# A decode-and-prefill layer on one core: the sample's sequences spread over the prompt's attention at every tenth half block in place of every eighth

## The chip, the cores and the metric

The kernel runs on one NeuronCore of a Trainium2 chip. The metric is the device time of one execution in microseconds (us). TensorE, VectorE, ScalarE and GpSimd have a queue each and work it off in program order; SyncE issues most of the transfers. They are tied to each other by semaphores only.

## The reference, cut to what matters

One layer of a hybrid decoder is applied to a prompt (1 sequence of 2048 tokens) and to a sample (8 sequences of 4 new tokens, each with a cache of keys and values). Only the attention is touched by the change. For the prompt:

```
for window, dilation in ((128, 1), (512, 4), (2048, 16)):
    # queries of one residue class, 128 at a time, against the 128 keys before and their own 128
    sc = einsum(q_block, k_window) * dh ** -0.5, masked to the band
    m = max(sc); p = exp(sc - m); l = sum(p); o = (p / l) @ v_window
outs of the three configurations merged by softmax of their log-sums
```

For each of the 8 sample sequences, the 4 new queries of 8 heads see, in the same three configurations, 129 strided keys each:

```
kg, vg = k_all[:, idx], v_all[:, idx]
sc = einsum('bthd,btjhd->bthj', q, kg) * dh ** -0.5
lse = logsumexp(sc); p = exp(sc - lse)
outs.append(einsum('bthj,btjhd->bthd', p, vg))
```

Around it stand the input projection and the RWKV-7 mixing (before), and the output projection, the mixture of experts and the final norm (behind).

## The kernel before, in words

The stages run one behind another. `attention` (L1266) is the third. Its prompt part has 48 blocks of 128 queries: 16 of dilation 1, 16 of dilation 4 (four residue classes of four), 16 of dilation 16 (sixteen classes of one). A block is done in two halves of four heads each, so there are 96 half blocks, u = 0 to 95. The first block of a class has no keys before it, and its halves use 128 keys in place of 256; from u = 64 on all are such small ones.

In a step u TensorE does: the scores of half block u+2 (`score`, L1474), the turning of the exponentials of u (`turn_p`, L1494), the weighting of u-1 by the values (`weigh`, L1508 and L1509), up to u = 26 in even steps a turning of the prompt's keys (`turn_x`, L1456), and in odd steps what there is of the sample (`sample`). VectorE does: mask and extremum of u+2 (`mask_min`, L1667), half of the copy of u's turned exponentials (`p_copy`, L1675), the sample's part. ScalarE does: exponentials of u+1 (L1576), the other half of the copy (L1583), the copy of the output of u-1 (L1590), the sample's exponentials and the issue of most of its transfers (`sample_loads`, L1602). In odd steps TensorE waits in `sample(u)` for both copies of u.

A sequence b of the sample is tied to the half block `at(b) = first_at + period * b`, with `first_at` 13:

- GpSimd multiplies keys and queries in three products (L1425, tiles `att_s_prd` and `ahead_feat` in turn: two buffers). Product i waits until the head sum i-2 has read its buffer.
- VectorE's head sums (L1698) stand at u = at(b)-6, -5 and -3, scale and mask (L1702) at -1.
- TensorE turns the scores at at(b) (L1518), VectorE takes the maxima, ScalarE the exponentials.
- TensorE turns the exponentials back at at(b)+4 (L1522, L1523), VectorE copies them (L1722, L1723), GpSimd spreads them over the nine key tiles (`by_tile`, L1433, tile `att_s_lm`).
- TensorE weighs the values at at(b)+6 (`weigh_sample`): 18 passes of L1529, 128 rows by 512 columns, and 2 of L1530 with 4 rows. VectorE keeps each head's own columns (L1727, L1729).
- The values of b are loaded by ScalarE's queue at at(b+1)-9, -8 and -7, the keys of b+1 at at(b)-6, -4 and -2, its queries at at(b)-5.

GpSimd's queue is written in this order:

```
for b in range(B):
    for j in range(3):
        product(b, j)
    if b >= 1:
        by_tile(b - 1)
by_tile(B - 1)
```

and TensorE's weighing waits for the values and for `by_tile`:

```
pe.wait_ge(sv_ld, 64 * b + 64)
pe.wait_ge(s_lm, b + 1)
```

The first turning of half block u behind a sample's step (`turn_p`) waits until VectorE has read the shared PSUM bank `t_ps[1]`. SyncE stores the sample's results at block (at(b) + 11) // 2.

Of the kernel before, what the change touches and what calls it, by code (L numbers as in the profile page):

```python
# [1265 lines left out]
def attention(nc, X, QT, ident, mask, spare, x_ld, q_ld, c_in, k_in, v_in, qkv_s, cache_k, cache_v, masks_s, o_out, m_out, os_out, ms_out):  # L1266
# [6 lines left out]
    NU = 2 * NBK  # L1273
    NV, NX, NO, NSC = 5, len(X), 3, 3
    B, N = cache_k.shape[0], cache_k.shape[1]
    at_new, first_at, period = 7, 13, 8
    at = lambda b: first_at + period * b
    with ExitStack() as ctx:
        sb = lambda n, s: ctx.enter_context(nc.sbuf_tensor(f"att_{n}", s, F32))
# [1476 lines left out]
def hybrid_layer(nc, a, consts, outs):  # L2756
# [34 lines left out]
                att_X, att_QT[:], att_ident[:], att_mask[:], kc_p, qt_p, ident, consts["band"], att_x_ld, att_q_ld, att_c_in)  # L2791
    clear_semaphores(nc)
    attention(nc, att_X, att_QT, att_ident, att_mask, rwkv_F[0], att_x_ld, att_q_ld, att_c_in, kc_p, vc_p, qkv_s, a["cache_att_k"], a["cache_att_v"], consts["sample"], o_p, m_p, o_s, m_s)
    early.close()
    clear_semaphores(nc)
# [50 lines left out]
```

## Time and profile before

| | |
|---|---|
| median of 3 runs | 3448.79 us (3446.48 to 3475.65) |
| the profiled execution | 3453.1 us, span of its instructions 3451.3 us |
| TensorE busy (matmul) | 3146.2 us, 91% |
| VectorE, ScalarE, GpSimd busy | 1318.3, 1013.0, 338.4 us |
| mean granted clock of TensorE | 0.951 |
| attention stage | about 1579 to 2036 us |

Times below are counted from the span's start. The durations and waits come from the one profiled execution, so they are set against its 3453.1 us. A granted clock of 1.00 is 2.4 GHz, 0.50 is 1.2 GHz. TensorE's matmuls overlap a little in the records, so the start of the next group is the safer end of a group. Every fp32 matmul is recorded as two passes, a turning (transpose) as one.

### The profile page before, as it was taken

Reading aid. Unit: us, or ns where it says so; the run is one execution under the profiler, and the core shown is the slowest. Engines: PE = TensorE matmul, PEld = TensorE weight load, DVE = VectorE, ACT = ScalarE, POOL = GpSimd, SP = SyncE. Lnnn points to the kernel's source line nnn. Section 1 sums busy time; section 2 is a strip of 40 time slices with the busy share of each in tenths; the row PEclk is TensorE's granted clock in tenths of the full one; section 3 lists DMA queues with packets and bytes.
Section 4 is the critical chain, followed back from the end, with each engine's and each line's share of the span. In section 5 each row is a group of like instructions: output and inputs, shape, how many; then the busy total and the mean of one; then the engine's idle time right before and its main releaser. Section 6 shows DMA issues by size and latency. Waiting matters only on the chain. (4 is left out here: it accounts for less than half of the span.)

```text
span 3451.3 us, 74888 instructions
## 1 busy us (share of the span) xinstructions
PE 3146.2 (91%) x30921; PEld 2149.7 (62%) x30922; DVE 1318.3 (38%) x3229; ACT 1013.0 (29%) x2151; POOL 338.4 (10%) x351
## 2 busy tenths in 40 slices
PE   6999999999859988988999979996999999999990
PEld 4667666676458888877767765554555555555550
DVE  3455344553224443435655436664111111111117
ACT  3334433344122222225544433331111111111112
POOL 0000000000110000003333000001101001010104
PEclk9999999999979999999999859997999999999995
DMA  6111111111273333326666446423768786677658
GB/s 209 63 71 65 51 46 63 70 55 45 72 180 113 120 137 120 119 98 204 183 182 179 125 162 193 154 80 123 278 242 284 239 283 223 227 277 245 233 193 306
DMA packets 299029, 544.42 MB, mean 158 GB/s; under 512 B 98146, under 2 KB 122466, under 8 KB 292116
## 3 DMA queue, kind: packets, MB, share of 16 engines
q1 hardware_dynamic: 252860, 401.29, 34.6%
q10 hardware_dynamic: 25128, 66.26, 6.1%
q0 software_dynamic: 20784, 73.15, 5.8%
q8 instruction: 197, 3.23, 0.4%
q14 instruction: 60, 0.49, 0.0%
HBM read 400.66 MB, written 139.98 MB: 157 GB/s over the span
## 5 line engine op out<-in xcount | busy, mean ns | idle before, releaser
L307 PE MATMUL proj_main_ps<-proj_xt,proj_w 128*128 128x257 f32 x1536 | 351.1, 381 | 0.0
L307 PEld LDWEIGHTS proj_main_ps<-proj_xt,proj_w 128*128 128x128 f32 x1536 | 290.2, 191 | 41.1
L2544 PE MATMUL moe_y_ps<-moe_w,moe_ht 128*64 128x512 f32 x1312 | 301.2, 601 | 3.1 <-ACT moe_ht L2583 3.1
L2292 PE MATMUL out_proj_ps<-out_w,out_ct 128*128 128x512 f32 x544 | 241.6, 598 | 6.1 <-DMA out_w<-in_w_out_dram 6.1
L337 PE MATMUL proj_main_ps<-proj_w,proj_xt 128*128 128x512 f32 x512 | 225.3, 593 | 0.0
L2594 ACT ACTIVATE moe_sg<-moe_gate 128x256 f32<-128x256 f32 x82 | 31.4, 383 | 535.7 <-PE moe_gate L2528 535.7
L2544 PEld LDWEIGHTS moe_y_ps<-moe_w,moe_ht 128*64 128x64 f32 x1312 | 87.3, 137 | 158.6 <-issue 155.3
L2292 PEld LDWEIGHTS out_proj_ps<-out_w,out_ct 128*128 128x128 f32 x544 | 101.7, 192 | 121.8 <-issue 120.5
L2630 DVE COPY moe_y<-moe_y_ps 128x512 f32<-128x512 f32 x82 | 56.7, 691 | 313.8 <-PE moe_y_ps L2544 313.8
L1190 DVE COPY_PREDICATED rwkv_t<-ahead_rwkv_cons,rwkv_level_ps 128x512 f32<-128x512 uint32 (+1 forms) x168 | 109.1, 660 | 175.7 <-PE rwkv_level_ps L908 175.4
L337 PEld LDWEIGHTS proj_main_ps<-proj_w,proj_xt 128*128 128x128 f32 x512 | 97.2, 190 | 108.4 <-issue 107.0
L1667 DVE CUSTOM_DVE_ANT_0 att_sc<-att_s_ps,ahead_mask 128x256 f32<-128x256 f32 (+1 forms) x384 | 117.2, 361 | 118.4 <-PE att_s_ps L1474 118.4
L908 PE MATMUL rwkv_level_ps<-rwkv_t,rwkv_w 64*64 64x64 f32 x2688 | 153.2, 221 | 2.7 <-issue 2.7
L2528 PE MATMUL moe_up<-moe_w,moe_xt 128*64 128x256 f32 x1344 | 154.3, 382 | 0.0
L2528 PE MATMUL moe_gate<-moe_w,moe_xt 128*64 128x256 f32 x1344 | 152.2, 379 | 0.0
L2579 ACT COPY moe_xt<-moe_xt_ps 128x512 f32<-128x512 f32 x83 | 48.6, 585 | 343.4 <-PE moe_xt_ps L2521 343.4
L2528 PE MATMUL moe_gate<-kept_first_gate,moe_xt 128*64 128x256 f32 x1280 | 147.5, 384 | 1.4 <-ACT moe_xt L2579 1.4
L2528 PE MATMUL moe_up<-kept_first_up,moe_xt 128*64 128x256 f32 x1280 | 146.9, 382 | 0.0
L1576 ACT ACTIVATE att_sc<-att_sc,att_nm 128x256 f32<-128x256 f32 (+1 forms) x384 | 145.6, 451 | 3.9 <-issue 3.1
L1509 PE MATMUL att_o_ps<-att_v,att_pt 128*128 128x65 f32 x768 | 142.0, 301 | 0.0
L2636 DVE TENSOR_TENSOR moe_hd<-moe_sg,moe_gate 128x256 f32<-128x256 f32 x82 | 34.6, 421 | 280.0 <-ACT moe_sg L2594 280.0
L1474 PE MATMUL att_s_ps<-att_kt,ahead_qt 64*128 64x256 f32 (+1 forms) x768 | 139.8, 493 | 0.9 <-DVE att_pt L1675 0.5
(362 smaller groups left out, 5535.3 us busy)
## 6 DMA issues: line engine op xcount, KB each, us to landing
moe_w<-in_expert_w_dram SPq DMA_DIRECT2D x64, 2048.0 KB, 9.6
y_rows<-rwkv_zero POOLq DMA_DIRECT2D x65, 512.0 KB, 4.8
kept_first_gate<-in_expert_w_dram SPq DMA_DIRECT2D x16, 2048.0 KB, 9.6
kept_first_up<-in_expert_w_dram SPq DMA_DIRECT2D x16, 2048.0 KB, 14.9
y_rows<-moe_y ACTq DMA_DIRECT2D x164, 128.0 KB, 6.0
ft_p<-proj_uf SPq DMA_DIRECT2D x32, 642.0 KB, 3.2
rwkv_feat<-ft_p SPq DMA_DIRECT2D x12, 1284.0 KB, 6.9
att_s_k<-in_cache_att_k_dram ACTq DMA_DIRECT2D x14, 1024.0 KB, 6.8
```

The lines of the kernel that those rows point to most:

```text
L307: last = mm(out[:, 0:w + 1], W[:, k, kind * C + m * P:kind * C + (m + 1) * P], XT[n % 2][:, k, 0:w + 1], start=(k == 0), stop=(k == KT - 1))
L337: last = mm(out[:], XT[n % 2][:, k, 1 + i // 2 * P:1 + (i // 2 + 1) * P], W[:, k, j * C:(j + 1) * C], start=(k == 0), stop=(k == KT - 1))
L908: last = mm(level_ps[g][part(c), hh * P + DH:(hh + 1) * P], W[g][part(c), hh, :], T[i % 3][part(c), h, DH:P], start=True, stop=True, skip_ ...
L1190: v.copy_predicated(T[i % 3][:, 4 * g:4 * g + 4, k0:P], wide(level(l)[:, k0:P], 4).bitcast(U32), four(level_ps[g][:])[:, :, k0:P]).then_in ...
L1474: last = mm(s_ps[u % 2][e][:, pl * 2 * P + k_from(u):(pl + 1) * 2 * P], QT[rows, q, q_at:q_at + d * (P - 1) + 1:d], KT[rows, q, k_at:k_at ...
L1509: last = mm(out, PT[u % 2][:, hl, 1, :], V[n % NV][:, h, :], start=first(u), stop=True, skip_group_check=True)
L1576: nc.scalar.activation(SC[u % NSC][:, hl, k0:], SC[u % NSC][:, hl, k0:], ACT.Exp, bias=NM[:, n, 4 * half + hl:4 * half + hl + 1], scale=-1 ...
L1667: v.tensor_tensor_reduce(SC[u % NSC][:, hl, k0:], s_ps[u % 2][e][:, pl * 2 * P + k0:(pl + 1) * 2 * P], mask[:, k0:], 1.0, 3e38, ALU.add, A ...
L2292: last = mm(proj_ps[j][:], CT[t % 2][:, k, :], W[:, k, 512 * j:512 * (j + 1)], start=(k == 0), stop=(k == KT - 1))
L2528: last = mm(bank[j * HB:(j + 1) * HB, 0:HF], XT[:, q, r * HB:(r + 1) * HB], W[:, k, j * HF:(j + 1) * HF], start=(k == 0), stop=(k == KT - ...
L2544: last = mm(py[j * HB:(j + 1) * HB, :], HT[:, c, r * HB:(r + 1) * HB], W2[s][:, k, j * 512:(j + 1) * 512], start=(k == 0), stop=(k == FE / ...
L2630: v.tensor_copy(Y[:], py[:]).then_inc(y_ev, 1)
```

## The change

One number in `attention`: the sequences are tied to half blocks 13, 23, ..., 83 in place of 13, 21, ..., 69. Everything that is placed by `at(b)` on the four engines and in the transfer queues moves with it; the last weighing goes from half block 75 to 89, and the last store of the sample's results from block 40 to block 47, the last one.

```
@@ -1273,7 +1273,7 @@
     NU = 2 * NBK
     NV, NX, NO, NSC = 5, len(X), 3, 3
     B, N = cache_k.shape[0], cache_k.shape[1]
-    at_new, first_at, period = 7, 13, 8
+    at_new, first_at, period = 7, 13, 10
     at = lambda b: first_at + period * b
```

## Rows read from the trace of the kernel before

**Rows 1.** Windows: us; busy PE, PEld, DVE, ACT, POOL; granted clock; DMA share; GB/s.

```profile
1598.90:1963.80 364.90, 361.33 (x2334) 269.00 (x2334) 217.46 (x753) 185.70 (x467) 122.88 (x32) 1.00 0.62 183
1964.00:2066.20 102.20, 78.53 (x389) 69.61 (x389) 41.01 (x201) 42.30 (x122) 0.95 (x1) 0.50 0.42 136
1938.98:1946.76 7.78, 7.78 (x62) 6.95 (x62) 3.81 (x30) 6.31 (x21) 0.00 (x0) 1.00 0.95 320
1966.85:2028.01 61.16, 61.16 (x322) 55.69 (x322) 21.72 (x144) 30.74 (x96) 0.00 (x0) 0.50 0.24 67
1775.53:1819.89 44.36, 43.89 (x258) 31.17 (x256) 24.73 (x84) 20.22 (x52) 15.64 (x4) 1.00 0.63 180
```

**Rows 2.** TensorE's timeline around the last sequence: start us, us, line, output<-inputs, passes.

```profile
1947.37 0.25 PE L1523 MATMUL att_t_ps<-ahead_ident,att_s_p 96*4 96x96 f32 x1
...
1952.73 7.97 PE L1529 MATMUL att_t_ps<-att_s_v,att_s_lm 128*96 128x512 f32 x18
1960.63 1.09 PE L1530 MATMUL att_t_ps<-att_s_vn,att_s_pn 4*96 4x512 f32 x2
1961.65 1.23 PE L1474 MATMUL att_s_ps<-att_kt,ahead_qt 64*128 64x128 f32 x8
...
2032.68 3.51 PE L1509 MATMUL att_o_ps<-att_v,att_pt 128*128 128x65 f32 x16
```

**Rows 3.** GpSimd's timeline, 1860 to 1970 us; in brackets its idle time before.

```profile
1911.49 4.55 POOL L1425 TENSOR_TENSOR att_s_prd<-att_s_k,att_s_q 128x2048 f32<-128x2048 f32 x1 [23.57 <-DVE att_s_sc L1698]
1917.08 2.03 POOL L1433 TENSOR_TENSOR att_s_lm<-att_s_pb,att_s_masks 128x864 f32<-128x864 f32 x1 [1.03 <-DVE att_s_pn L1723]
1948.14 2.03 POOL L1433 TENSOR_TENSOR att_s_lm<-att_s_pb,att_s_masks 128x864 f32<-128x864 f32 x1 [29.03 <-DVE att_s_pn L1723]
```

**Rows 4.** VectorE's timeline, 1900 to 1970 us.

```profile
1909.07 2.28 DVE L1698 TENSOR_REDUCE att_s_sc<-att_s_prd 128x32 f32<-128x2048 f32 x1
...
1947.83 0.23 DVE L1723 COPY att_s_pn<-att_t_ps 4x96 f32<-4x96 f32 x1
...
1961.76 0.69 DVE L1727 TENSOR_TENSOR att_s_om<-att_t_ps,att_s_masks 96x512 f32<-96x512 f32 x1 [9.08 <-PE att_t_ps L1530]
1962.48 1.06 DVE L1729 TENSOR_REDUCE att_s_o<-att_s_om 96x64 f32<-96x512 f32 x1
```

**Rows 5.** TensorE's timeline from turning back to weighing, and steps between.

```profile
1658.39 0.25 PE L1523 MATMUL att_t_ps<-ahead_ident,att_s_p 96*4 96x96 f32 x1
...
1666.56 1.91 PE L1529 MATMUL att_t_ps<-att_s_v,att_s_lm 128*96 128x512 f32 x4
...
1720.89 1.14 PE L1474 MATMUL att_s_ps<-att_kt,ahead_qt 64*128 64x256 f32 x8
1724.62 0.27 PE L1518 MATMUL att_t_ps<-ahead_ident,att_s_sc 128*96 128x128 f32 x1
...
1728.81 1.30 PE L1474 MATMUL att_s_ps<-att_kt,ahead_qt 64*128 64x128 f32 x8
1732.80 0.83 PE L1474 MATMUL att_s_ps<-att_kt,ahead_qt 64*128 64x256 f32 x2
...
1874.56 0.24 PE L1523 MATMUL att_t_ps<-ahead_ident,att_s_p 96*4 96x96 f32 x1
...
1883.51 1.05 PE L1529 MATMUL att_t_ps<-att_s_v,att_s_lm 128*96 128x512 f32 x2
```

**Rows 6.** Transfers of the sample's keys: issue to landing.

```profile
DMA to landing us min/median/max: 2.6/7.7/12.0
...
att_s_k<-in_cache_att_k_dram ACTq DMA_DIRECT2D x14, 1024.0 KB, 6.8
```

**Rows 7.** TensorE's waits, 1580 to 2040 us (us, times, longest); the output projection's first passes.

```profile
PE att_t_ps L1522 <- DVE att_pt L1675: 1.9, 4, 0.5
PE att_t_ps L1529 <- DVE att_pt L1675: 0.7, 1, 0.7
...
2061.80 4.61 PE L2292 MATMUL out_proj_ps<-out_w,out_ct 128*128 128x512 f32 x5 [5.12 <-DMA out_w<-in_w_out_dram]
```

More of the change, by code:

```diff
@@ L1275, in attention @@
     B, N = cache_k.shape[0], cache_k.shape[1]
-    at_new, first_at, period = 7, 13, 8
+    at_new, first_at, period = 7, 13, 10
     at = lambda b: first_at + period * b
```

## The prediction

> **What bounds the kernel now.** I read the busy time by windows first, for the attention stage alone, since no other stage is touched. From 1598.9 to 1963.8 us TensorE is busy 361.33 of 364.90 us at a granted clock of 1.00, that is 2.4 GHz; from 1964.0 to 2066.2 it is granted 0.50, 1.2 GHz [rows 1]. So the stage costs what TensorE's queue holds, and two things can change its length: waits that enter that queue, and the stretch at half clock. A half block of the dilation-16 part (half blocks 64 to 95, all of them first blocks with 128 keys) takes 7.78 / 3 = 2.59 us at 2.4 GHz and 61.16 / 16 = 3.82 us at 1.2 GHz, with TensorE busy all the time in both, while VectorE has 1.27 us of work in one [rows 1]. A period of eight half blocks in the dilation-4 part takes 44.36 us, with a sequence in it [rows 1]. Then TensorE's timeline around the last sequence shows the order of work and where the clock falls: the weighing (18 passes over cached values, 2 over the new ones) starts at 1952.73 and ends at 1961.65, and the half blocks behind it go at the lower clock [rows 2]. Last come the queues of GpSimd and VectorE, which feed the weighing [rows 3, 4].
>
> **What the change does, part by part.**
>
> *Nothing is added or removed.* The same instructions run. Sequence b has its scores turned at half block 13+10b in place of 13+8b, its probabilities turned back 4 later, its weighing 6 later. Three things change: (1) sequences 5, 6 and 7 are weighed at 69, 79 and 89, where before only the last two stood among small half blocks, at 67 and 75; (2) work of neighbouring sequences meets in a new order; (3) the 19 half blocks behind the last weighing shrink to 6.
>
> *The new order, and the wait it makes.* VectorE's head sums stay at 6, 5 and 3 half blocks ahead of a sequence's turning, so the first sum of sequence b+1 moves from 2 half blocks behind the turning of b to 4 behind: the same half block in which the probabilities of b are copied, and only two ahead of the weighing of b. GpSimd's queue is in program order: third product of b+1, then the spreading of b's probabilities by tile (L1433), on which b's weighing waits. The third product shares its buffer with the first, so it waits for the first sum. Before, this product came 3 us or more ahead of the copied probabilities: in the last case it started at 1911.49, the spreading at 1917.08 [rows 3]. Now the chain behind the turning back is: start of the second turning to the end of VectorE's second copy 1947.83 + 0.23 - 1947.37 = 0.69; the head sum 2.28; 0.14 to GpSimd's start (sum at 1909.07, product at 1911.49); the product 4.55; the spreading 2.03, taken as starting at once; some 0.1 to TensorE. That is 9.8 us [rows 2 to 4]. Against it stands what TensorE has to do in two half blocks. Between that turning and the weighing lie 1666.56 - 1658.39 = 8.17 us in the dilation-1 part with an input turned, 1883.51 - 1874.56 = 8.95 at half blocks 57 to 59, and 1952.73 - 1947.37 = 5.36 among the small ones [rows 2, 5]. For sequence 1 (27 to 29) no input is turned any more: two halves of 3.8 (1720.89 to 1724.62 is 3.73) and 0.2, 7.8 us; for sequence 2 two halves of 3.99 (1728.81 to 1732.80) and 0.2, 8.2 us; for sequence 3 it is about 8.2 too, from the same matmuls in another order [rows 5]. So waits: 1.6, 2.0, 1.6, 1.6, 0.85 for sequences 0 to 4, 7.7 us together; 9.8 - 5.4 = 4.4 us for sequence 5; for sequence 6 also 4.4, or 9.8 - 0.2 - 2 x 3.82 = 1.9 if its half blocks run at half clock. Sequence 7 has no follower: its spreading starts at once, as before, and ends in 0.8 + 2.0 us: no wait.
>
> *Who stands behind it.* On TensorE the scores, turnings and weightings of all later half blocks; ScalarE and VectorE then wait for those with room to spare. ScalarE's loads wait on products and weighings that lie four or more half blocks back, so they hold nobody. The load of b's last values moves from 5 to 3 half blocks ahead of its weighing. Its landing is not in the trace; keys of the same size land in 6.8 us (median), the slowest transfer of that buffer took 12.0 [rows 6]. Among large half blocks 12 us pass, among small ones 8 plus the 4.4 just found, for sequence 7 some 7.7 us. I take nothing (the value near the median), with 0 to 4 us as bounds.
>
> *Small waits that go and come.* TensorE waited four times 0.47 us for VectorE's copy behind a head sum at half blocks 33, 41, 49 and 57, and 0.72 us ahead of the weighing at 67 [rows 7]. The sums now lie elsewhere or under the longer wait: -2.6 us. New ones: the third sum now comes right behind the weighing. Among small half blocks VectorE then has 0.69 + 1.05 of the weighing's result, twice 1.27 of its own and 2.28 of the sum, 6.6 us, against 2 x 2.59 = 5.2 of TensorE: 1.3 us each at 70/71 and at 80/81 [rows 1, 3, 4]. +2.6 us; at half clock nothing. The nearest row, one sum alone, cost 0.72, so I keep 1.4 to 2.6.
>
> *The clock.* Before, half blocks 77 to 92 ran at 1.2 GHz: 61.16 - 16 x 2.59 = 19.7 us, and some 3.5 us more to the last weighting, 23.2 us in all [rows 1, 2]. What did the engine do before the clock fell at 1963.9? It had ended the dense weighing, run two passes with only 4 rows, and gone on with score matmuls on 64 rows. The same small half blocks had run at 2.4 GHz between the two last weighings [rows 1], and they did not bring it back either in the 70 us behind. It came back only in the output projection, 4.5 us after that had begun passes of 512 columns back to back, each then taking about 0.9 us (five in 4.61) against 7.97 / 18 = 0.44 [rows 2, 7]. From this I take: a wait of 1.3 to 4.4 us among small half blocks lets the clock fall more surely than that seam did; it then stays low until the next weighing, which starts at 1.2 GHz, runs its first 4.5 us so (+2.2 us) and brings 2.4 back. Likeliest course: down at the wait ahead of 69, up in weighing 5, down at 71, up in weighing 6, down at 81, up in weighing 7, and no wait behind that. Half blocks at half clock are 72 to 79 and 82 to 89: 16 x 1.23 = 19.7 us. Behind the last weighing none (bounds: none, or six, +7.4).
>
> The page "TensorE: Matmul & The Clock Gate" of the Trainium skill, section "HAM oscillation — how this bites in real kernels", says that waits between short bursts of matmuls put the engine back to the low clock and that each next burst starts cold. The trace bears it out between stages only; inside the stretch at 1.00 no wait of these is longer than 0.7 us [rows 7]. By that rule all seven waits would cost such a start, the second rival below.
>
> **Sum.** Waits for the spreading 7.7 + 4.4 + 1.9 = +14.0; VectorE's lag +2.6; waits gone -2.6; cold starts of three weighings +6.6; half clock +19.7 - 23.2 = -3.5. Total +17 us. The profiled execution took 3453.1 us (span 3451.3, 1.8 around it), 4.3 above the median 3448.8 of the runs shown, so 3470 on its scale and 3466 on the median's. I forecast 3465.
>
> **Rivals.**
> 1. *Forecast, the clock falls in both gaps between the last weighings:* 3465. For it: waits of over 1 us at 69, 71, 81. Chance 0.45.
> 2. *The waits bring the clock down among large half blocks too.* Each of the five weighings 0 to 4 then starts at 1.2 GHz, 5 x 2.2 = +11, and with late values or six slow half blocks at the end, up to +18: 3476 to 3483. Against it: the four waits of 0.47 us there left 1.00. Chance 0.17.
> 3. *One of the two gaps keeps 2.4 GHz:* -9.8 of half clock, -2.2 for the next start, +2.5 of longer wait: 3456. Chance 0.22.
> 4. *Other side: not slower.* Both gaps keep 2.4 GHz. Then the 23.2 us are won whole and paid with 7.7 + 8.8 + 2.6 - 2.6 + 2.2: -4.5, 3444. It decides by whether 1.3 us of wait at 71 and 81 suffice to bring the clock down; if the lag is 0.7, the seen size, it may not. Chance 0.11.
> 5. *GpSimd's chain is no limit* because the spreading comes in time after all. Then 16 us of waits go and only the clock speaks: -15 to -20, 3431. Against it stands the program order and the buffer's wait. Chance 0.05.
>
> **How the numbers follow.** A change of 1% is 34 us, about what tells from none here. Cases 1, 3, 4, 5 and most of 2 lie within it. Slower by more needs case 2 with everything against it: 0.06. Faster by more needs 3414: 0.02. The rest, 0.92, is no change. The range takes in cases 1 to 4, from 3440 to 3482.
>
> **What would show it.** TensorE's busy time up to 1963 falls short by some 8 us more than before; matmuls of L1529 wait for GpSimd's att_s_lm, seven times, over 4 us once or twice; GpSimd's spreading stands right behind a product seven times; the mean clock of the stage shows several short stretches at 0.50 in place of one of 102 us; behind the weighing at 89 half blocks last 2.6 us. The forecast is wrong if the clock holds between 69 and 89, or falls in every large wait, or if L1529 waits for a transfer.

## The result, and the profile after

The changed kernel takes 3488.33 us (median of 10 executions, 3479.16 to 3494.31); the kernel before, on the same chip, 3448.2 (10 executions, 3437.85 to 3475.65). The ratio is 1.0106, with an interval of 1.0078 to 1.0134: slower by 1%, and above the forecast range. The profiled execution of the changed kernel took 3493.5 us, span 3491.7, mean granted clock 0.949. In what follows one execution of the kernel before (4947.94 us) and one of the version with the passes in the middle (4889.38 us), both at a mean granted clock of 0.61, are left out of every median and count.

The attention stage, from its first matmul on `att_t_ps` to its last on `att_o_ps`, now takes 475.4 us (1600.2 to 2075.6) in place of 456.8 (1579.4 to 2036.2). It begins 20.8 us later, though no instruction ahead of it changed.

TensorE's waits by line from 1580 to 2080 us (us in all, times, longest), which answer to [rows 7]:

```profile
PE att_t_ps L1529 <- POOL att_s_lm L1433: 11.4, 7, 4.0
...
PE att_s_ps L1474 <- DVE att_pt L1675: 3.4, 4, 1.3
...
PE att_t_ps L1522 <- DVE att_pt L1675: 0.5, 1, 0.5
```

The forecast wait is there, seven times, and the four waits of L1522 have become one. Two of the four at L1474 are VectorE's lag at half blocks 71 and 81 (1.25 and 1.23 us), the others are 0.5 us. The timeline around the weighing of sequence 5 (start, us, engine, line; idle time before in brackets) shows the chain link by link:

```profile
1942.17 0.23 DVE L1723 COPY att_s_pn<-att_t_ps 4x96 f32<-4x96 f32 x1
1942.34 2.26 DVE L1698 TENSOR_REDUCE att_s_sc<-ahead_feat 128x32 f32<-128x2048 f32 x1
1944.74 4.54 POOL L1425 TENSOR_TENSOR ahead_feat<-att_s_k,att_s_q 128x2048 f32<-128x2048 f32 x1 [20.95 <-DVE att_s_sc L1698]
1949.23 2.01 POOL L1433 TENSOR_TENSOR att_s_lm<-att_s_pb,att_s_masks 128x864 f32<-128x864 f32 x1
1951.39 9.63 PE L1529 MATMUL att_t_ps<-att_s_v,att_s_lm 128*96 128x512 f32 x18 [4.00 <-POOL att_s_lm L1433]
1960.96 1.09 PE L1530 MATMUL att_t_ps<-att_s_vn,att_s_pn 4*96 4x512 f32 x2
...
1964.97 2.27 DVE L1698 TENSOR_REDUCE att_s_sc<-ahead_feat 128x32 f32<-128x2048 f32 x1
...
1968.47 1.25 PE L1474 MATMUL att_s_ps<-att_kt,ahead_qt 64*128 64x128 f32 x8 [1.25 <-DVE att_pt L1675]
...
2001.44 10.28 PE L1529 MATMUL att_t_ps<-att_s_v,att_s_lm 128*96 128x512 f32 x18 [1.81 <-POOL att_s_lm L1433]
```

The probabilities of sequence 5 are copied at 1942.4. The head sum takes VectorE until 1944.6, the third product GpSimd until 1949.3, and only then come the spreading and the weighing. The sum at 1964.97 makes VectorE late by 1.25 us at half block 71. Both weighings take longer than the 7.97 us of [rows 2].

Windows (us; busy PE, PEld, DVE, ACT, POOL; granted clock; DMA share; GB/s), against [rows 1]:

```profile
1619.30:1951.50 332.20, 318.66 (x2132) 244.53 (x2132) 192.64 (x672) 173.65 (x426) 105.03 (x27) 0.99 0.58 175
1951.70:1968.40 16.70, 15.52 (x60) 7.94 (x58) 6.28 (x21) 3.43 (x11) 5.52 (x2) 0.90 0.38 122
1968.70:2006.10 37.40, 35.59 (x169) 29.59 (x170) 16.90 (x81) 16.16 (x51) 9.74 (x3) 0.50 0.51 148
2006.30:2019.70 13.40, 12.17 (x59) 7.20 (x59) 6.27 (x21) 3.84 (x12) 0.00 (x0) 1.00 0.14 40
2019.90:2053.90 34.00, 34.00 (x166) 28.72 (x163) 12.22 (x79) 16.02 (x50) 2.02 (x1) 0.50 0.48 135
2054.10:2077.80 23.70, 21.06 (x128) 15.06 (x126) 7.58 (x40) 9.34 (x29) 0.00 (x0) 1.00 0.17 47
...
1970.79:1990.11 19.32, 19.32 (x103) 17.48 (x103) 8.40 (x51) 10.13 (x32) 1.12 (x1) 0.50 0.58 150
```

The course is the forecast one. It runs: 2.4 GHz before weighing 5, 3.4 us of 1.2 GHz at its start, 2.4 again, 1.2 from half block 71 into weighing 6, 2.4 behind it, 1.2 again from 81 into weighing 7, 2.4 to the end. Five half blocks at the low clock take 19.32 us, 3.86 each.

So the profile shows the forecast mechanism, and yet the time is 23 us off. The experiments look for where the 23 us come from.

### The profile page after: what moved, and what is told of

The parts are those of the page before. It is cut to its first block and busy times, and to the rows that moved or that the text cites. A ratio compares the mean times of both kernels' runs of the same rounds, so it can differ in the third digit from the quotient of the medians.

```text
span 3491.7 us, 74888 instructions
## 1 busy us (share of the span) xinstructions
PE 3155.7 (90%) x30921; PEld 2152.9 (62%) x30922; DVE 1317.1 (38%) x3229; ACT 1014.2 (29%) x2151; POOL 339.1 (10%) x351
## 5 line engine op out<-in xcount | busy, mean ns | idle before, releaser
L1474 PE MATMUL att_s_ps<-att_kt,ahead_qt 64*128 64x256 f32 (+1 forms) x768 | 139.3, 492 | 3.8 <-DVE att_pt L1675 3.4
L1118 ACT COPY rwkv_w<-rwkv_level_ps 128x256 f32<-128x256 f32 x168 | 62.7, 373 | 264.9 <-PE rwkv_level_ps L894 259.0
```

Source lines behind the costliest of these rows:

```text
L1118: nc.scalar.copy(W[g][:].rearrange("p h k -> p (h k)"), level_ps[g][:, 0:4 * DH]).then_inc(w_copied[g], 1)
L1474: last = mm(s_ps[u % 2][e][:, pl * 2 * P + k_from(u):(pl + 1) * 2 * P], QT[rows, q, q_at:q_at + d * (P - 1) + 1:d], KT[rows, q, k_at:k_at ...
```

## The experiments

Each ratio is against the kernel before, on the same chip and measured beside it. The experiments were made in three batches, each on another chip, so each version is compared with its own batch's kernel before: the first four runs (29 executions of the kernel before), the next four (34) and the last three (25). A stage length is that of the one profiled execution, counted from the first matmul on `att_t_ps`; the expectations of the first four count it from a later point and so have 448 and 468 us for what is 456.8 and 475.4 here.

### The two kernels once more

No edit. If the part ahead of the stage is slow by chance, a second pair must come closer together; if the change makes it slow, it must be slow again.

**The kernel before.** 

> The kernel before, unchanged, run again as if it were a new kernel. The changed kernel's trace is 40 us longer: 20 us of it lie in the attention stage, as forecast, and 20 us ahead of it, where not one instruction differs. Theory A (chance of an execution: the clock falls a different number of times in the RWKV stage, and the seam between projection and RWKV is of different length): this run's first exponentials of the attention stage start anywhere from 1580 to 1610 us, and its runs scatter over 3438 to 3476 around 3448. Theory B (something systematic of the changed program acts ahead of the stage): attention starts here within 3 us of before (1588 at the first copy), and the ratio to before is 1.000.

**The changed kernel.** 

> The changed kernel, unchanged, run again. Theory A (chance): its attention stage is 20 us longer than before's (448 to 468 us), but the part ahead of it comes out anew, between 1580 and 1610 us, and over more runs the ratio to before goes down towards 1.006 (20 us). Theory B (systematic): the part ahead is again 15 to 20 us longer than before's, and the ratio is again 1.010 to 1.012 (35 to 40 us).

Measured: before again 3438.02 us, ratio 0.9995 (0.9958 to 1.0033); changed again 3478.47 us, ratio 1.011 (1.0062 to 1.0158). The ratio repeats, while the part ahead of the stage doesn't: the stage begins at 1576.1 and 1582.4 us in the two profiles, against 1579.4 and 1600.2 in the first pair. Each theory had one half right: the start came out anew, as A had it, and the ratio stayed, as B had it. So neither explains it. What differs between the two profiles of one and the same kernel is the attention stage of the kernel before: 456.8 us at first, 434.4 now. The changed kernel's is 475.4 and 475.0.

The page's row of the granted clock (40 slices of the span, tenths of 2.4 GHz), the kernel before, first profile:

```profile
PEclk9999999999979999999999859997999999999995
```

and the kernel before again:

```profile
PEclk9999999999979999999999989997999999999995
```

Slice 23 (counted from 0, each 86.3 us) holds the end of the stage: 5 in place of 8. The long fall of [rows 1] is not there the second time. In the windows of that execution the last half blocks run at 1.00:

```profile
1598.90:1963.80 364.90, 361.32 (x2320) 269.03 (x2320) 217.17 (x755) 184.99 (x466) 120.59 (x31) 1.00 0.61 181
1964.11:2005.59 41.48, 41.48 (x322) 36.97 (x322) 20.32 (x145) 30.75 (x97) 0.00 (x0) 1.00 0.38 99
```

41.48 us for the 16 half blocks 77 to 92 are 2.59 each, where the first profile had 61.16 us. The kernel is the same, and the same seam stands ahead of them. In the stretch before it TensorE is busy 361.32 us here and 361.33 there.

How often is it so? Only two executions of the kernel before have a profile, but each has its mean granted clock beside its time. Of 88 in the three batches, 56 have 0.953 or more, with a median of 3436.9 us, and 32 have less, with 3458.6; by batch the lower clock is in 9 of 29, 12 of 34 and 11 of 25, and it is in 3 of the 12 executions of this experiment itself, which the 88 leave out. The difference of 21.6 us is about the stage's own (456.8 - 434.4 = 22.4). The clocks fit too: behind 1963.8 us the first profile has 102.6 us at 0.50 and the second 27.4, and (102.6 - 27.4) x 0.5 / 3440 = 0.011; the two groups' median clocks are 0.959 and 0.949. That the group of lower clock is the fall at the end is inferred from these sums, not seen in each execution. The cut at 0.953, made with the values in view, is not sharp: 12 of the 88 lie from 0.951 to 0.955, and the groups' times overlap from 3448.6 to 3454.6 us. The changed kernel's six of this batch lie at 0.945 to 0.950, the first ten at 0.945 to 0.952. A third theory: *the kernel before loses its last stretch in about one execution of three, the changed kernel loses its two stretches in every one, and the profile from which I forecast was one of the three.* The next experiments test that, and which edit mends what.

### Spreading ahead of the third product (changed kernel)

```
-                for j in range(3):
+                for j in range(2):
                     product(b, j)
                 if b >= 1:
                     by_tile(b - 1)
+                product(b, 2)
```

> Period ten, but in GpSimd's queue the spreading of sequence b stands ahead of the third product of b+1, so it need not wait for the head sum and that product. Theory of the prediction (the waits come from this order): the seven waits ahead of the weighings go (14 us at the clocks seen), the clock no longer falls at half block 69, and the attention stage gets 10 to 20 us shorter than the changed kernel's 468 us; the clock between the weighings may still fall behind VectorE's lag at 71 and 81. Rival (the wait is for the values or for VectorE's copies): the stage keeps 468 us within 4 and the waits ahead of L1529 stay.

Measured: 3468.08 us, ratio 1.0084 (1.0056 to 1.0111); stage 465.4 us. TensorE's waits in the stage, with lines shifted by one by the edit:

```profile
PE att_t_ps L1530 <- DVE att_pt L1676: 3.5, 3, 1.8
PE att_s_ps L1475 <- DVE att_pt L1676: 3.4, 4, 1.3
```

The waits for the spreading are gone, all 11.4 us; in their place TensorE waits three times for VectorE's copies (L1530), 3.5 us in all. The stage is some 10 us shorter (465.4 against 475.0 and 475.4), at the lower edge of the expectation. The clock still falls for 3.5 us at the start of weighing 5, behind a wait of 1.81, where it was expected to stay at 2.4 GHz, and comes back in that weighing. VectorE's lag behind the late sums stays (L1475), and so do the two long falls: 34.1 us from 1934.2 and again from 1982.0. Each begins within 0.7 us of the end of a lag:

```profile
1933.57 1.25 PE L1475 MATMUL att_s_ps<-att_kt,ahead_qt 64*128 64x128 f32 x8 [1.25 <-DVE att_pt L1676]
```

A lag of 1.25 us is enough for a long fall; the wait for GpSimd isn't needed.

### The period of eight, only later (kernel before)

```
-    at_new, first_at, period = 7, 13, 8
+    at_new, first_at, period = 7, 27, 8
```

> Period eight as before, but the first sequence at half block 27, so the last weighing stands at 89 as in the changed kernel, without the new order of spreading and head sums. Theory (the seam behind a weighing or a wait among small half blocks brings the clock down, the next weighing brings it back): four weighings (65, 73, 81, 89) stand among small half blocks, the low clock behind the last one is 6 half blocks or none in place of 19, with up to 8 slow half blocks in each gap; if the clock holds in the gaps the stage is 15 to 20 us shorter than before's 448 us, if it falls in every gap about as long (445 to 455). Rival (the length of the tail at half clock does not matter, only the waits do): the stage stays at 448 within 3 whatever the clock shows.

Measured: 3447.69 us, ratio 1.0008 (0.998 to 1.0036); stage 448.0 us, in a profiled execution that took 3455.3 us and so is among the slower ones. On the expectation's own count that is some 440 us, between its two cases. The last weighing is at 89 as in the changed kernel, but the order of work between neighbours is the old one. There is no wait for the spreading; yet the clock is down for 51 us of the stage in all, 6.8 of it from 1934.6, two microseconds behind a wait of 1.50 us for VectorE, and 30.7 from 1951.7 into the weighing at 81, behind which it holds 2.4 GHz to the end:

```profile
1932.43 0.30 PE L1522 MATMUL att_t_ps<-ahead_ident,att_s_p 96*128 96x96 f32 x1 [1.50 <-DVE att_pt L1675]
...
1948.37 1.09 PE L1530 MATMUL att_t_ps<-att_s_vn,att_s_pn 4*96 4x512 f32 x2
1949.39 1.23 PE L1474 MATMUL att_s_ps<-att_kt,ahead_qt 64*128 64x128 f32 x8
```

A weighing at 89 doesn't by itself make the kernel slow. And the second fall has no wait right ahead of it: it begins, as in [rows 2], some 2 us behind the two passes with 4 rows that end a weighing. Behind the same two passes at 81 and 89 nothing fell. They became the next suspect.

### The head sums moved, the period of ten kept (changed kernel)

```
                 for b in range(B):
-                    for g in range(3):
-                        if u == at(b) - (6, 5, 3)[g]:
+                    if u == at(b) - 4:
+                        head_sums(b, 2)
+                for b in range(B):
+                    for g in range(2):
+                        if u == at(b) - (8, 6)[g]:
                             head_sums(b, g)
```

> Period ten with GpSimd's queue as it is, but VectorE's head sums moved: the first two to 8 and 6 half blocks ahead of the turning (odd steps, one each), the third into the weighing of the sequence before, ahead of its result. Theory (the changed kernel's stage is 475 us because of the spreading's wait, VectorE's lag at 67/69, 70/71 and 80/81, and the falls of the clock that they set off): all of it goes, the stage takes 430 to 436 us like the undisturbed stage of before, sometimes 10 us more when the clock falls at the seam of weighing 5 or 6; ratio to before 0.995 to 1.002. Rival (small half blocks with a period of ten cannot hold 2.4 GHz between weighings, whatever waits there are): no waits, but the clock still falls around 71 and 81 and the stage stays above 450 us.

Measured: 3453.99 us, ratio 1.0035 (1.0011 to 1.006); stage 444.2 us with some 14 at the low clock. Both the stage (430 to 436) and the ratio (0.995 to 1.002) miss the expectation, though nothing of its rival came. Against the changed kernel the ratio falls by 0.0075, some 26 us, for moving three VectorE instructions per sequence; the stage of the profiled execution, 31 us shorter, is from the fastest of the twelve (3444.07 us). Neither the wait for GpSimd nor the lag is left (of L1474's waits two of 0.5 us remain), and with them the two long falls are gone. Part of the miss is a wait that the forecast had bounded at 0 to 4 us:

```profile
PE att_t_ps L1529 <- issue: 5.2, 3, 3.0
```

"issue" means that the trace names no releaser. What else L1529 waits for are the values; the last version below tests it. Behind the longest of the three the clock is down for 3.5 us. Another part is a wait of 1.99 us at the turning of an input (L1456, "issue"), 0.63 in the kernel before.

### The four-row passes in the middle of the weighing (kernel before)

In the kernel before, the two passes over the new values (4 rows) stand between the weighing and the scores of the next half block. Here they go behind the fifth of the nine key tiles, the same passes into the same sum.

```
                 for i in range(NT):
-                    mm(... SV[:, i, :], start=(i == 0), stop=False)
-                mm(... PN[:], VN[:], start=False, stop=True).then_inc(s_weighted, 1)
+                    last = mm(... SV[:, i, :], start=(i == 0), stop=(i == NT - 1))
+                    if i == 4:
+                        mm(... PN[:], VN[:], start=False, stop=False)
+                last.then_inc(s_weighted, 1)
```

> The kernel before, but the two passes with 4 rows stand in the middle of the weighing (behind five of nine value tiles), not at its end. Same work. Theory (before falls in one of three executions, because the end of the last weighing is a seam of one us of 4-row passes followed by 64-row scores, and it stays low behind it for want of a weighing): the fall disappears; no run in the upper group, all within 3425 to 3445, median 3435, mean 8 us below before's. Rival (the fall has another cause, such as the small half blocks themselves): the upper group around 3460 stays, in a quarter or more of the runs.

Measured: 3432.5 us, ratio 0.9959 (0.9936 to 0.9983); stage 438.1 us. A window behind the last weighing, 338 passes where 16 half blocks have 322:

```profile
1964.50:2008.00 43.50, 43.46 (x338) 38.78 (x337) 21.58 (x153) 32.11 (x101) 0.00 (x0) 1.00 0.38 100
```

All 11 executions lie between 3425 and 3442 us at a clock of 0.958 or more: the group of low clock has gone, as expected. If it still came in 12 of 34, as in the kernel before of this batch, 11 without one would come about 8 times in 1000 ((22/34)^11). No instruction was added or taken away, so what decided it was where these two passes stand. Short falls elsewhere stay: 6.8 us from 1829.0 in this profile, 2.7 us behind a wait of 0.48, as in the kernel before again (3.4 us from 1739.7, behind a wait of 0.47). It is the fastest version of the study and beats both kernels.

### A longer seam (kernel before)

The opposite edit: two more matmuls (four passes) over the new values ahead of the last one, for the last sequence alone, whose new values are thereby counted three times.

```
+                for _ in range(2 if b == B - 1 else 0):
+                    mm(... PN[:], VN[:], start=False, stop=False)
                 mm(... PN[:], VN[:], start=False, stop=True).then_inc(s_weighted, 1)
```

> The kernel before, but the 4-row passes of the last weighing (half block 75) are done three times, 2 us more; the last sequence's new values count threefold. Theory (a stretch of little work for TensorE at this seam brings the clock down for all of the 19 half blocks behind, when it falls so that the chip sees it): with 3 us in place of 1 it is seen always or nearly so: nearly all runs in the upper group, 3450 to 3470, ratio 1.004 to 1.009, stage 457 to 460 us. Rival (upper group by chance, whatever stands at the seam): the share of upper runs stays between a quarter and a half, and the median rises by 2 us.

Measured: 3460.26 us, ratio 1.0046 (1.0022 to 1.0069), stage 460.6 us, with all 12 executions at a clock of 0.952 or less; with the 11 of 25 of this batch's kernel before, 12 of 12 would come by chance about 5 times in 100,000 ((11/25)^12). TensorE's timeline and the window behind it:

```profile
1966.33 1.95 PE L1531 MATMUL att_t_ps<-att_s_vn,att_s_pn 4*96 4x512 f32 x4
1968.12 1.02 PE L1532 MATMUL att_t_ps<-att_s_vn,att_s_pn 4*96 4x512 f32 x2
1969.07 1.25 PE L1474 MATMUL att_s_ps<-att_kt,ahead_qt 64*128 64x128 f32 x8
```

```profile
1969.30:2044.50 75.20, 75.20 (x392) 68.97 (x392) 26.73 (x166) 36.02 (x112) 0.00 (x0) 0.50 0.22 62
```

TensorE isn't idle anywhere here (75.20 of 75.20 us), and its clock is halved all the same. With a seam of 0 us none of 11 executions is in the group of low clock, with 1 us about one in three, with 3 us all 12. That bears out the third theory for the kernel before: the fall at its last seam is drawn anew in every execution. What decides a draw, the runs don't show.

### The same placement in the changed kernel

The edit of the placement in the middle, on the changed kernel.

> The changed kernel with nothing but the 4-row passes in the middle of the weighing. Theory (in the changed kernel the clock falls behind VectorE's lag at 71 and 81 and in the waits, not at the seam): nothing changes, stage 473 to 477 us, ratio to before 1.008 to 1.013. Rival (the seam brings it down there too): the stage gets 10 us or more shorter, as it did in the mean for the kernel before.

Measured: 3476.01 us, ratio 1.0082 (1.0053 to 1.0111); stage 478.9 us (473 to 477 was expected; three short falls of 3.4 to 6.8 us stand ahead), the falls at 1945.1 (37.5 us) and 1996.3 (34.1 us), each again within 0.8 us of the end of a lag (1.25 and 1.23 us), and still this wait:

```profile
PE att_t_ps L1529 <- POOL att_s_lm L1433: 10.8, 6, 4.0
```

Here the falls don't come from the seam. Of the edits tried only the sums' order removes them.

### Both edits together, at ten and at eight

Sums moved and four-row passes in the middle. At a period of eight the first two sums stand at `at(b) - (6, 4)[g]` and the third at `at(b) - 2`.

**At ten.** 

> Period ten with both: sums moved and 4-row passes in the middle. Theory: no waits, no falls within the stage: 430 to 434 us, all runs in one group, at or a little under before's lower group (3425 to 3442), ratio 0.993 to 0.999. Rival (gaps of ten small half blocks fall by themselves): stage above 450 us.

**At eight.** 

> Period eight with both: sums at 6 and 4 ahead and the third into the weighing. Theory: before's small waits (2.6 us) go as well, the stage takes 431 to 433 us and no run is in the upper group: ratio 0.992 to 0.998, the same as period ten with both within 2 us, so the period as such is worth nothing. Rival (spreading wider is a gain or a loss of its own): the two differ by more than 5 us.

Measured: at ten 3449.66 us, ratio 1.0014 (0.9992 to 1.0037), stage 446.2; at eight 3436.61 us, ratio 0.9972 (0.9949 to 0.9995), stage 441.1. At ten stage and ratio miss the expectation, and the two differ by 13 us, which was the rival's mark. No long fall is left in either profile; at ten the executions' clocks run from 0.956 to 0.960, with the sums moved alone from 0.951 to 0.960, so some draws at the seams may have gone with it, which no profile shows. At eight moving the sums gained nothing over the placement in the middle alone (438.1): the four waits of 0.47 us at L1522 stayed (1.9 us), and L1456 now waits four times, 2.8 us in all, for something the trace doesn't name.

What holds the version at ten is seen in its timeline. The values of sequence 6 are issued by ScalarE's queue (ACTq) three half blocks ahead:

```profile
1951.92 0.33 ACTq L1604 DMA_DIRECT2D att_s_v<-in_cache_att_v_dram  x1
1952.29 0.37 ACTq L1616 DMA_DIRECT2D att_s_vn<-qkv_s  x1
1956.02 2.02 POOL L1433 TENSOR_TENSOR att_s_lm<-att_s_pb,att_s_masks 128x864 f32<-128x864 f32 x1
1965.28 5.18 PE L1529 MATMUL att_t_ps<-att_s_v,att_s_lm 128*96 128x512 f32 x6 [5.05 <-issue]
```

```profile
1945.00:1960.00 15.00, 14.79 (x118) 12.96 (x114) 12.34 (x59) 11.56 (x37) 6.54 (x2) 1.00 0.91 175
1960.00:1965.00 5.00, 0.23 (x3) 0.09 (x1) 2.05 (x1) 1.55 (x5) 0.00 (x0) 0.83 0.94 301
```

The spreading is done at 1958.0, and the weighing starts 7.2 us later, 13 us after the issue, with the transfer engines 0.91 and 0.94 busy. That nothing but the values is left is argued; the next kernel tests it.

### The values two half blocks earlier as well

On top of the version at ten:

```
-                            if u == at(b) - (9, 8, 7)[g]:
+                            if u == at(b) - (11, 10, 9)[g]:
                                 load_sample_v(b - 1, g)
```

> Period ten with the sums moved and the 4-row passes in the middle, and the sample's values loaded two half blocks earlier (5 ahead of the weighing, as with period eight, in place of 3). In the run without this TensorE stood 5.1 us ahead of the weighing at 79 and 1.8 us at 89, with no engine named. Theory (it waited for the values): these waits go, the stage goes from 446 to 434 to 440 us, ratio to before below 1. Rival (the wait is another one, such as a semaphore of GpSimd): the waits and the 446 us stay.

Measured: 3441.15 us, ratio 0.998 (0.9957 to 1.0003); stage 443.9 us. The unnamed wait of L1529 is gone, so it was the values'. The ratio falls from 1.0014 to 0.998, within the two intervals. The stage missed its expectation of 434 to 440 us, for another reason: the clock was at 1.2 GHz early in it.

```profile
1615.50:1629.20 13.70, 13.24 (x59) 11.11 (x59) 7.57 (x22) 5.44 (x12) 5.35 (x2) 0.50 0.71 244
```

```profile
1615.96 1.09 PE L1456 MATMUL att_t_ps<-ahead_ident,ahead_x 128*128 128x128 f32 x4 [1.99 <-issue]
```

The fall begins in the wait of 1.99 us at the turning of an input, which the moved sums at ten all have. With the sums moved alone it brought 3.5 us of low clock, with both edits none. At ten with everything mended the ratio is 0.998, at eight with both edits 0.9972: the intervals overlap. A difference between the periods as such doesn't show above them (some 8 us each way); what the change cost was the order of work it made.

## Why the prediction was wrong, step by step

**What bounds the kernel, nothing added or removed:** right. The stage is still TensorE's queue and its clock.

**The waits for the spreading:** forecast +14.0 us; measured 11.4 under L1529. Weighing 0 waited 0.3 (forecast 1.6), with 0.9 more at the turning of an input just ahead; weighings 1 to 4 waited 1.8, 1.5, 1.5 and 0.6 (2.0, 1.6, 1.6 and 0.85), weighing 5 4.0 (4.4), weighing 6 1.8 (1.9). Moving the sums and moving the spreading each removed it.

**VectorE's lag at 71 and 81:** forecast 1.3 us each (6.6 - 5.2 is 1.4), measured 1.25 and 1.23. That it brings the clock down was forecast and came, in both profiles of the changed kernel and in two experiments that kept it. **Small waits gone:** 2.6 forecast. L1522 and L1529 lost 2.1, but as much came new at L1518 (0.9), L1474 (0.5) and L1456 (0.9): in sum nothing.

**Cold starts of weighings:** forecast 3 x 2.2. The 18 passes of weighings 5, 6 and 7 took 9.63, 10.28 and 9.83 us, against 7.97 in [rows 2]: 5.8 us; weighing 1 was slow too, 9.49, in this profile. **Half clock between the weighings:** forecast 16 half blocks at 3.82; measured 71.4 us at 0.50 in two windows, as drawn. The Trainium skill, page "TensorE: Matmul & The Clock Gate", section "HAM oscillation — how this bites in real kernels", says that waits between short bursts send the next burst off cold; its example has waits of some 3 to 5 us, so the forecast's step to all seven waits here, of 0.3 to 4.0 us, goes further than the page. The trace agrees among the small half blocks, in both gaps: a long fall stands behind each lag. At weighing 1 the clock fell for 3.4 us behind a wait of 1.80, but in the second profile of the changed kernel it did not, and the kernel before again has such a fall at half block 33, behind a wait of 0.47. At the other large ones the trace doesn't agree: the window shows 0.99. So of the rivals the first was the course that came, and the others didn't.

**Values' transfers:** taken 0, bounds 0 to 4. No wait for them shows in the changed kernel, so 0 there; up to 5.1 us once the longer wait was gone.

**The step that failed** is the last term of the clock's part, "23.2 us in all", the half clock that the kernel before would have and the changed one be rid of. I read it from one execution and credited it to every one. It is a draw at a seam of 1 us: by the clocks, 32 of 88 executions have it. In the majority the kernel before pays nothing there, and nothing can be won back. On the profiled execution's own stage the sum was good: +17 us forecast, 475.4 - 456.8 = +18.6 measured. Against the stage that most executions have it is 475.4 - 434.4 = 41.0 us, and the medians differ by 3478.5 - 3439.1 = 39.4 in the batch whose clocks are on record. In the forecast's own terms: +17 plus 23.2 that wasn't there to win gives +40.

The first pair's medians differ by 40.1 as well, 3488.3 - 3448.2. There the account is less complete: the ten executions of the kernel before have no clock on record, and both kernels took 9 to 10 us more than in the next batch, which no run explains.

Two things should have warned me. The mechanism I wrote down for the fall (two passes of four rows, then short scores) had stood behind weighing 6 as well, where the same half blocks held 2.4 GHz [rows 1]: a cause that acts once and not the other time is no fixed term. And the shown runs spread from 3446 to 3476 us. The right range would have had a second centre some 22 us higher.

The profiled executions of the first pair differ by 40.4 us in span, which looks like the same number but isn't the same thing: 18.6 of it are the stage, and 20.8 lie ahead, 14.3 of them in the RWKV stage. From its first matmul to the attention's, before and then after:

```profile
982.31:1579.43 597.12, 521.34 (x16121) 497.99 (x16121) 225.71 (x429) 156.22 (x357) 54.85 (x91) 0.95 0.34 124
```

```profile
988.76:1600.22 611.46, 529.64 (x16121) 506.02 (x16121) 225.06 (x429) 156.39 (x357) 54.85 (x91) 0.94 0.33 121
```

The same 16121 passes take longer at a little lower clock. In the second profile of the changed kernel the stage took 599.7 us, in the kernel before again 591.7, and over the eleven experiments it lies between 589.6 and 602.6, in versions at ten (589.6 to 601.6) as in those at eight (591.7 to 602.6). So no systematic difference shows; the 611.5 is the highest of all thirteen.

## What to carry to other kernels

Before crediting a change with the removal of something seen in a profile, ask whether it is in every execution: put the mean granted clock of all executions beside their times, and if they form two groups, forecast from both. Check in the same way whether the profiled execution is a typical one. Where the period of a software pipeline is changed, draw the queues of the helpers anew: constant offsets keep the distance to their own sequence and change that to the neighbour, and a sum on VectorE that another engine's product waits for can then stand ahead of what TensorE needs next. Among short half blocks put small passes inside a dense group, not between it and the next short ones: in the kernel before that was worth 0.4%.

## What the runs showed of the hardware

- The granted clock of TensorE fell to 1.2 GHz without any idle time: a seam of 1.02 us of four-row passes in front of score matmuls on 64 rows at the end of the last weighing had it behind it in one of two profiles and, by the mean clock of each execution, in 32 of 88; with 3 us of such passes it was there in 12 of 12, with none in 0 of 11. TensorE counts as fully busy in such a stretch (75.20 of 75.20 us).
- Among small half blocks a wait of 1.23 to 1.25 us was followed by 1.2 GHz within 0.8 us in all eight cases of four profiles, and the clock came back only in the next weighing, 34 to 38 us later. Waits of 0.5 to 2 us among large half blocks were mostly followed by nothing, at times by 3.4 to 13.7 us of low clock.
- The short matmuls of a small half block can keep 2.4 GHz (41.48 us at 1.00), and at 1.2 GHz they did not win it back (75.20 us at 0.50).
- One and the same program has its executions in two groups 21.6 us apart, told by the mean clock (cut at 0.953), and one profile shows one of the two.
- A sequence's last values, issued 13 us ahead, were not there in time while the transfer engines were 0.91 to 0.94 busy (5.05 us of wait, gone when they were issued two half blocks earlier); the keys' median from issue to landing was 6.8 us, and 6.0 in the changed kernel.
